# A two-block forward pass on one core: x loaded first, and six shift blocks instead of four on TensorE

## The reference, cut to what matters

```
mod = silu(c) @ w_ada + b_ada          # 9 pieces of 1024: sh1, sc1, g1, sh2, ...
u   = rmsnorm(x, norm_ff1) * (1 + sc1) + sh1
h   = x + 0.5 * g1 * (silu(u @ w_gate) * (u @ w_up)) @ w_down
...                                     # token mixing, second FFN, second block with mixer,
                                        # cross attention and a PEER layer that gathers 256 x 128 expert rows
```

## Time and profile before

| | us |
|---|---|
| median of 3 runs | 1695.32 |
| the three runs | 1691.71, 1695.32, 1695.86 |
| profiled execution, its own time | 1699.18 |
| span of the profiled execution | 1697.9 |
| PE busy | 1525.4 (90%) |
| DVE busy | 1064.4 (63%) |
| ACT busy | 713.7 (42%) |
| mean granted TensorE clock | 0.964 |

### The profile page before, as it was taken

The page is one execution under the profiler, slowest core; times in us unless marked ns, Lnnn a source line. Parts: engine busy times, 40 slices in busy tenths (PEclk is TensorE's granted clock), DMA queues, the critical chain, the costliest instruction groups (busy, mean ns, idle before and its releaser), DMA issues.

```text
span 1697.9 us, 21606 instructions
## 1 busy us (share of the span) xinstructions
PE 1525.4 (90%) x7972; PEld 1131.8 (67%) x7972; DVE 1064.4 (63%) x1944; ACT 713.7 (42%) x1561; POOL 354.9 (21%) x325
## 2 busy tenths in 40 slices
PE   6999989998989998798999997988988898788786
PEld 5899988888889998797997774544533343344222
DVE  5666675775655555668564135767777777676754
ACT  4534345344344444544342124434444444444443
POOL 0200010000010001001100013444444444444451
PEclk9999999899999999798999999999999999999999
DMA  8877756555555553332233539999999999999996
GB/s 315 326 253 264 242 191 237 203 201 196 190 179 188 184 188 134 100 125 75 100 113 112 223 101 379 364 420 422 421 421 421 421 422 421 421 422 421 422 421 263
DMA packets 91002, 463.66 MB, mean 273 GB/s; under 512 B 10769, under 2 KB 10929, under 8 KB 57873
## 3 DMA queue, kind: packets, MB, share of 16 engines
q0 software_dynamic: 39216, 277.05, 39.9%
q1 hardware_dynamic: 50688, 183.52, 31.1%
q10 hardware_dynamic: 992, 1.71, 0.3%
HBM read 460.15 MB, written 2.10 MB: 272 GB/s over the span
## 4 chain that ended last, share of the span: by engine, by line
PE 60%; DMA 20%; DVE 10%; ACT 6%; issue 3%; POOL 0%; ACTq 0%; SPq 0%; DVEq 0%; POOLq 0%
DMA Ft<-peer_uv,ids 12%; PE ps L1277 10%; PE ps L497 7%; PE ps L498 7%; PE ps L499 7%; DMA uhi<-peer_uv,ids 4%; PE ps L1098 3%; DMA mlo<-peer_uv,ids 3%; PE ps L622 2%; PE ps L623 2%; PE ps L624 2%; DVE Ft L2061 2%; PE ps L1180 2%; PE ps L541 2%; DVE wlo L1302 2%
## 5 line engine op out<-in xcount | busy, mean ns | idle before, releaser
L1277 PE MATMUL ps<-Ft 128*128 128x512 f32 x792 | 387.8, 625 | 79.1 <-ACT Ft L2607 78.2
L1277 PEld LDWEIGHTS ps<-Ft 128*128 128x128 f32 x792 | 146.9, 197 | 297.1 <-ACT Ft L2607 161.8
L2061 DVE CUSTOM_DVE_ANT_0 Ft<-Ft 128x1024 f32<-128x1024 f32 x198 | 242.7, 1226 | 145.3 <-DMA Ft<-peer_uv,ids 136.8
L1302 DVE TENSOR_TENSOR wlo<-raw,whi 128x1024 fp32r<-128x1024 f32 x228 | 278.1, 1245 | 82.2 <-ACT whi L2085 81.9
L497 PE MATMUL ps<-uhi,whi 128*128 128x256 f32 x1088 | 314.6, 289 | 6.5 <-DVE ulo L1453 4.5
L498 PE MATMUL ps<-ulo,whi 128*128 128x256 f32 x1088 | 310.6, 285 | 0.0
L499 PE MATMUL ps<-uhi,wlo 128*128 128x256 f32 x1088 | 310.4, 285 | 0.0
L2735 POOL DMA_INDIRECT Ft<-peer_uv,ids x198 | 223.1, 1127 | 296.8 <-PE ps L1277 268.0
L2085 ACT ACTIVATE whi<-raw 128x1024 fp32r<-128x1024 f32 x228 | 229.5, 1047 | 17.5 <-PE ps L543 7.7
L497 PEld LDWEIGHTS ps<-uhi,whi 128*128 128x128 f32 x1088 | 211.8, 195 | 10.9 <-DVE ulo L1453 4.9
L498 PEld LDWEIGHTS ps<-ulo,whi 128*128 128x128 f32 x1088 | 211.6, 194 | 1.9 <-issue 0.5
(11 more groups left out here) (433 smaller groups left out, 2313.4 us busy)
## 6 DMA issues: line engine op xcount, KB each, us to landing
raw<-ff_gu SPq DMA_DIRECT2D x88, 512.0 KB, 4.7
raw<-w_ada SPq DMA_DIRECT2D x56, 512.0 KB, 4.8
raw<-ff_dn SPq DMA_DIRECT2D x44, 512.0 KB, 4.5
raw<-w_in SPq DMA_DIRECT2D x32, 512.0 KB, 3.6
raw<-w_in_s SPq DMA_DIRECT2D x28, 512.0 KB, 4.4
raw<-w_mod SPq DMA_DIRECT2D x16, 512.0 KB, 6.6
raw<-w_out SPq DMA_DIRECT2D x14, 512.0 KB, 4.4
raw<-w_in_m SPq DMA_DIRECT2D x12, 512.0 KB, 4.3
```

Of the source, the lines that this page charges most:

```text
L1277: ins = t.matmul(acc[r][c], diag[n % NDIAG], gbuf[SEAT[n]][:, 1024 + c * 512:1024 + (c + 1) * 512], start=False, stop=(n % 128 == 127))
L1302: v.tensor_tensor(lo, raw_slot(j), hi.bitcast(F32), ALU.subtract).then_inc(*up("lo", j))
L2061: v.tensor_tensor_reduce(pjunk, gbuf[SEAT[n]][:, 0:1024], xn[:, q // 8, :], 1.0, 0.0, ALU.mult, ALU.add, dots[:, n:n + 1]).then_inc(*up("d ...
```

## The change

Three things. First, the queue of ACT loads x right behind c, ahead of the row, the bias and the norm weights. Second, the split of the second tile moves: on ACT its high part is written ahead of the squares, on DVE its remainder is written ahead of `mean_square`. Third, `NMOD` goes from 4 to 6, so DVE loses the totals of shift blocks 4 and 5 and TensorE gets `first_shift(4)` and `first_shift(5)`; and TensorE's order, which was shifts 0, 1, 2, four groups of transposes, shift 3, becomes shifts 0, 1, two groups of transposes, shift 2, two groups of transposes, shifts 3, 4, 5. SP's waits follow `NMOD`: the slots of shift blocks 4 and 5 are now freed by TensorE.

```
-NMOD = 4
+NMOD = 6

-        def norm_start(name, src, by=1):
+        def norm_start(name, src, by=1, between=None):
...
                 ins.then_inc(*up("tr", name, q))
+                if q == 1 and between:
+                    between()
...
             if which == 0:
-                for k in range(3):
+                first_shift(0)
+                first_shift(1)
+                norm_start(name, h, 2, lambda: first_shift(2))
+                for k in range(3, NMOD):
                     first_shift(k)
-                norm_start(name, h, 2)
-                first_shift(3)
...
             gain(0)
+            lows(cur.upto(mod_at[0, 1] - 1))
             mean_square("ff1")
-            lows(cur.upto(mod_at[0, 1] - 1))
             gain(1)
...
             highs(cur.upto(0))
+            highs(cur.upto(mod_at[0, 1] - 1))
             a.wait_ge(*at("x"))
             squares("ff1", h)
-            highs(cur.upto(mod_at[0, 1] - 1))
...
         a.dma_start(cc, D["c"]).then_inc(*land("cc"))
+        a.dma_start(h, D["x"].rearrange("(r p) n -> p r n", p=128)).then_inc(*land("x"))
         a.dma_start(crow, bc(D["c_row"], [128, 1024])).then_inc(*land("crow"))
         a.dma_start(bcol, D["b_ada_col"]).then_inc(*land("bcol"))
         a.dma_start(vec, D["vecs"]).then_inc(*land("vec"))
-        a.dma_start(h, D["x"].rearrange("(r p) n -> p r n", p=128)).then_inc(*land("x"))
```

## The result

The changed kernel has a median of 1705.29 us over 20 runs (1697.23 to 1711.48). The kernel before, measured with it, has 1697.12 us over 20 runs (1691.71 to 1702.98). The ratio is 1.0043, 95% interval 1.0029 to 1.0056, so some 7.3 us slower by the ratio. The 20 runs lie in three heaps: five from 1697.2 to 1698.9, nine from 1703.6 to 1706.3, six from 1709.4 to 1711.5. I had forecast 1697.7 with a range that ended at 1703.4, and gave 0.25 to slower. The forecast was counted from 1695.3, the median of the first three runs of the kernel before; its 20 runs have a median 1.8 us higher, and that is most of the 1.9 us by which the result lies outside. As a difference I had 2.4 us, with 8.1 as the far end, and measured 7.3.

What follows compares the result with a forecast made beforehand. PE has work almost without a gap from the first group's end, so that end sets the rest; earlier transposes and mid-range clock times move it from 46.1 to 48.5, and 1695.3 + 2.4 = 1697.7 us, range 1691.5 to 1703.4.

Steps and rivals of the forecast that it cites:

- x first, second tile ahead: transposes at 21.0: First norm: x lands earlier, so PE's transposes start at 21.0 instead of 22.83, 1.8 us earlier (ends 0 and 2.5).
- one of my signs of being wrong: Prediction is wrong if the transposes (L480) do not start before 22 us.
- Nothing on PE from SP's later slots: SP's later w_mod issues cost PE nothing; at most 1 us if the cover by shift 2's transfer fails.
- Shifts and transposes, middle of each range, 48.5: PE up to the first group's end: middle of high and low clock times gives 48.5, 2.4 us later than 46.1.
- rival B: PE's clock stays low until the first group, which ends at 52.7, 6.6 us later: 1701.9 us; chance 0.25.
- the all-high case: PE's clock stays high through shifts 3 to 5; u decides, group ends at 44.3, 1.8 us earlier: 1693.5; chance 0.20.
- Whatever moves the end of the first group moves the rest by as much: PE waits only 0.3 us from the first group's end to 240 us, so only that point, 46.1 before, is compared.
- my last sign: Prediction is wrong if the difference at the first Silu isn't the difference at the end.
- The same step, at the buckets: Bucket products behind the first group: the first group's delay was to carry through unchanged, with no extra size given.
- Two totals off DVE count as nothing: DVE's 2.5 us saved on shifts 4 and 5 return as a longer wait for w_mod; counted as nothing.
- my sum: Whole kernel: 2.4 us added to the median 1695.3 gives 1697.7; chance 0.45.

Runs made afterwards that it cites:

- the second profile: Profiled execution of the changed kernel timed once more, nothing altered: 1709.85 us, first Silu at 53.31; ratio 1.0034 to the kernel before.
- the first profile: Profiled execution of the changed kernel in its first measurement: 1703.89 us, first Silu at 47.56; ratio 1.0043 to the kernel before.
- the pair with restored banks: Changed kernel with thin or 128-column shift products, free PSUM bank list reset after the first FFN to the kernel before's order: ratios 1.0028 and 0.9994.
- the changed list: Kernel before, only its free PSUM bank list after the first FFN put in the changed kernel's order: ratio 1.0021.
- without the split: Changed kernel with shifts 0, 1, 2, four unbroken groups of transposes, then shifts 3, 4, 5: ratio 0.9996 to the kernel before.

## Why the prediction was wrong, step by step

- *x first, second tile ahead: transposes at 21.0.* Mis-sized. They start at 22.09 (21.55 in the second profile): 0.7 to 1.3 us earlier than before instead of 1.8. The term was within the ends I kept (0 to 2.5), but "not before 22" was one of my signs of being wrong, and the first profile shows it.
- *Nothing on PE from SP's later slots.* Right: with wide products in the same order PE waits 0.34 us for u and the first Silu is early.
- *Shifts and transposes, middle of each range, 48.5.* The mechanism was right: the clock at the shifts sets the end of the first group. In the first profile the terms are 1.84, 2.03 and 7.45 us where I took 2.7, 2.6 and 8.0, and the Silu came at 47.56. That it came near 48.5 is partly luck, since the second profile is rival B, 53.31 against my 52.7, and some one in three runs lies in its heap. My forecast lay 4.2 us above the all-high case (2.4 later against 1.8 earlier). The swap from thin to wide products is worth 0.0033 in one pair (1.0043 to 1.0010) and 0.0034 in the pair with restored banks (1.0028 to 0.9994), 5.6 to 5.8 us, so this term was too small by some 1.5 us.
- *"Whatever moves the end of the first group moves the rest by as much."* This is the step that failed, as my last sign said it would show: 1.4 us at the first Silu became 4.7 at the end of the first profile, and 7.2 became 10.7 in the second. I looked at PE's waits only up to 240 us, where they stayed as small as I said (0.4 us in both profiles), and at nothing of what the edit does to the bank list, which I put at nothing without naming it. On the kernel before the changed list by itself costs 0.0021, 3.6 us (interval 1.2 to 5.9). In the two pairs with and without it the difference is 0.0015 and 0.0016, 2.5 to 2.7 us, and there the intervals overlap.
- *The same step, at the buckets.* The time from the third to the fourth Silu is 13.6 us before and 15.5 in both profiles of the changed kernel, while the third Silu was 1.1 and 6.9 us late. It is not a fixed price of the change. It is 12.3 us with six shifts alone, 12.3 in the changed kernel with wide products and 15.5 in the same with restored banks, two programs that are alike up to there. The granted clock of the first of these two is 1.00 from 56 to 66 us, that of the second 0.50 from 59.8 to 66.4. The clock falls there in some executions and not in others, so this stretch adds to or takes from whatever the first Silu shows.
- *Two totals off DVE count as nothing.* Not tested by itself. The last w_mod pair was issued from 33.1 on, and u was never what PE waited for in the changed kernel up to the end of the first group.

In the terms of my sum, 2.4 was 4.2 for the clock less 1.8 for the earlier start. The measured 7.3 is 5.7 for the clock and 2.6 for the banks less 1.0 for what is left when both are gone (0.9994). That these three add up says nothing, because they are steps of one chain from 1.0043 to 1. What can be checked is that each part came out alike with and without the other. Each difference has an uncertainty of some 3.5 us. The clock's part is shown by two pairs of separate intervals, although the changed kernel's second ratio (1.0034, from 1.0012) would overlap the first pair. The cost of the list is shown on the kernel before; its size in the changed kernel is an estimate.

## What to carry to other kernels

Look at what kind of products a stretch of TensorE work holds, not only at how busy the engine looks. The clock's part here (5.6 to 5.8 us) was more than the 3.7 us that two more shifts take at the high level, and widening the products to 128 columns took it away. When resources are handed out by a rotating list, an edit in the prologue rewires waits hundreds of microseconds later, so compare the assignment of banks or buffers before and after, or pin it; and remember that an experiment which reorders the prologue changes the list too. Don't carry a delay at one point to the end without looking for places behind it where executions of one program differ. And where a cost has two values, forecast the two and how often each comes, not their mean.

## What the runs showed of the hardware

TensorE was busy without a gap for some 20 us in the second profile of the changed kernel (21.55 to past 42), and every shift and transpose in it ran at the low level (3.41 us a shift). The Trainium skill (page "TensorE: Matmul & The Clock Gate", section "Why this matters for your kernels") advises to keep TensorE continuously busy to reach the full clock. This trace does not agree, as far as the profile's busy time goes: in that stretch the shifts have one column a product, and with 128 columns at the same places the same order reached 1.95 us a shift. One column does not always bring the low level either: behind an unbroken run of transposes one shift took 1.84 us in the kernel before, and three took 5.42 without the split but 8.19 with six shifts alone. And a product of 128 columns costs little more than one of a single column: 1.95 against 1.84 us per 16 at the high level, 3.75 against 3.54 at the low one.
